# Two transformer layers with product-key experts: the down products with blocks of the v tile standing and 384 activations moving, and the gathered rows summed in SBUF

## The chip, the core and the metric

The kernel runs on one core of one Trainium2 chip. The metric is device time in microseconds (us) of that core, from launch to end; lower is better. The engines are TensorE (PE), VectorE (DVE), ScalarE (ACT), GpSimd (POOL) and SyncE (SP), the last of which only issues transfers here. A column is one element of the free dimension.

## What is computed

The reference is a trunk of two layers. In each layer a mixer sub-layer of three attention branches is followed by PEER, a retrieval of single-neuron experts. The change lies wholly in the last part of PEER. Cut to that:

```python
def peer_ffn(h, w_q, sub_keys, u_tab, v_tab):      # h: 512 tokens x 1024
    ...                       # per token: 8 heads x 16 experts of 16384, with weights g
    u = u_tab[experts]
    vv = v_tab[experts]
    a = gelu(einsum('td,ted->te', xb, u)) * g
    return einsum('te,ted->td', a, vv)
...
x = x + g2 * peer_ffn(...)                          # g2: one factor per model column
```

## The kernel before

The kernel treats the 512 tokens in two ways. For the first 128 tokens (`SPARSE`) it gathers the rows of the chosen experts, 128 a token, with indirect DMAs that POOL issues, and DVE does the arithmetic on them. For the other 384 (`DENSE`) it computes with all 16384 experts: the table comes in 128 tiles of 128 experts x 1024, and the activations, which are zero for experts that weren't chosen once the routing weights are multiplied in, go through PE.

The residual stream `xT` lies with the model dimension on partitions: 8 slices (`KT`) of 128, each with 512 token columns. PSUM has 8 banks of 512 float columns; `PS[4]` and `PS[5]` together are `pair`, which the profile calls `banks4and5`.

To keep precision, each operand of a product is split into a high part in fp32r and the remainder (`_hi`, `_lo`), and `product3` (lines 709 to 714) issues three products: high by high, and the two mixed ones. The helper's lines 712 to 714 are therefore the lines of all products in the profile, of the up stages (names `h_hi`, `u_hi`) and of the down stage (`a_hi`, `u_hi`; the v tiles use the same buffers as the u tiles, so `u_parts` holds v there). The first operand of `product3` is the one that stands in the array (128 partitions x 128 columns), the second the one that moves. In names of the profile and of the listings below, `bank<-moving,standing`.

In the up stages (`query`, `select`, `route`, `rest`) a column is one u tile: 8 slices x 3 products, with a 128x128 block of u standing and the 384 dense activations moving. The results go through Gelu on ACT and out to HBM. The stage `down` then has 16 steps of 8 tiles (`DOWN`), 128 tiles in all. For each tile:

- SP loads the v tile into a slot of `W`, and once per four tiles the activations (`act_in`) and routing weights (`g_cur`).
- ACT rounds the tile (`lead_down`, L1405) and the weighted activations (`round_weighted`, L1411).
- DVE multiplies the next activations by their weights (`weigh`, L2082), takes the remainder of the tile (`u_lo`, L2093), adds one gathered row per sparse token times its weight to a running sum (`sparse_down`, L2072; after it POOL may gather the next row into that place, L1551), and takes the remainder of the activations (`a_lo`, L2097).
- PE (`outputs`, from L1100) waits for both remainders, and issues for each of 3 token blocks x 2 halves of the model dimension one `product3`: 128 tokens stand and 512 columns of v move. The six results accumulate in banks 0 to 3, 6 and 7 (`DENSE_BANKS`) over all 128 tiles, with tokens on partitions.

Four tile buffers let DVE and ACT run ahead of PE by some blocks. The sparse sum lies in `pair`, banks 4 and 5, also with tokens on partitions; DVE clears it (L2060) before the stage.

After the last tile both results have to be turned, since `xT` has the model dimension on partitions. DVE copies the sparse sum to SBUF (L2106), ACT copies the six dense banks (L1446), PE turns 8 + 24 blocks of 128x128 (L1127 and L1135), and DVE adds each, times `g2`, to `xT` (`add_output`, L2110), in 32 instructions of 128 columns. Then all engines meet at a boundary and the next layer begins. The order on every engine is written out by hand; semaphores hold the engines together.

Of the kernel before, what the change touches and what calls it, by code (L numbers as in the profile page):

```python
# [40 lines left out]
ALU = mybir.AluOpType  # L41
ACT = mybir.ActivationFunctionType
# [4 lines left out]
D = 1024  # L47
# [166 lines left out]
def build_trunk(nc, x_t, stream, vecs, consts, c_t, gate_tiles, z_dram, tab_u, tab_v, u_rows, v_rows, out_t, route_dram, act_dram, layers=LAYERS):  # L214
# [3 lines left out]
    with ctx:  # L218
        def sb(name, shape, dt=F32):
            return ctx.enter_context(nc.sbuf_tensor(name, shape, dt))  # L220
# [144 lines left out]
        gathered_rows = sb("gathered_rows", [128, 6, D])  # L365

# [137 lines left out]
        sparse_copied = sem("sparse_copied")  # L504
        sparse_turned = sem("sparse_turned")
        y_ready = sem("y_ready")
        y_copied = sem("y_copied")
        y_turned = sem("y_turned")
# [91 lines left out]

        DENSE_BANKS = [0, 1, 2, 3, 6, 7]
# [104 lines left out]
        def _(pe):  # L706
# [244 lines left out]
            with pe.Fori(0, layers) as layer:  # L951
# [55 lines left out]
                if "experts" in stages:  # L1007
# [92 lines left out]
                    def outputs(step, first=False, last_step=False):  # L1100
                        for j in range(DOWN):
# [3 lines left out]
                            for i, bank in enumerate(DENSE_BANKS):  # L1105
                                t0, d0 = i // 2 * 128, i % 2 * 512
                                if opens and i == 0:
                                    pe.wait_ge(route_copied.sem, route_copied.at("route", layer, STEPS["route"] - 1, Q))
                                    pe.sem_inc(held, 1)
                                if opens and i == 4:  # L1110
                                    pe.wait_ge(col_read.sem, col_read.at("rest", layer, 0, 8))
                                    pe.sem_inc(held, 1)
                                last = product3(PS[bank][:], [a[:, j % 4, t0:t0 + 128] for a in a_parts],
                                                [v[:, j % 4, d0:d0 + 512] for v in u_parts], opens, ends)
                                if ends and i < 5:
                                    last.then_inc(y_ready, 1)
# [7 lines left out]
                    pe.wait_ge(sparse_copied, layer + 1)  # L1124
                    pe.sem_inc(held, 1)
                    for k in range(KT):
                        last = nc.tensor.transpose(pair[:, k * 128:(k + 1) * 128],  # L1127
                                                   gathered_rows[:, 0, k * 128:(k + 1) * 128], cst("ident"))
                    last.then_inc(sparse_turned, 1)
                    for i, bank in enumerate(DENSE_BANKS):  # L1130
                        pe.wait_ge(y_copied, layer * 6 + (i + 1))
                        pe.sem_inc(held, 1)
                        for c in range(4):
                            d0 = i % 2 * 512 + c * 128
                            last = nc.tensor.transpose(PS[bank][:, c * 128:(c + 1) * 128],  # L1135
                                                       gathered_rows[:, 1 + i // 2, d0:d0 + 128], cst("ident"))
                        last.then_inc(y_turned, 1)
# [3 lines left out]
        def _(act):  # L1141
# [127 lines left out]
            with act.Fori(0, layers) as layer:  # L1269
# [44 lines left out]
                if "experts" in stages:  # L1314
# [123 lines left out]
                    act.wait_ge(row_used.sem, row_used.at("summed", layer, STEPS["summed"] - 1, 8))  # L1438
                    act.sem_inc(held, 1)
                    for i, bank in enumerate(DENSE_BANKS):  # L1440
                        if i < 5:
                            act.wait_ge(y_ready, layer * 5 + (i + 1))
                        else:
                            act.wait_ge(col_done.sem, col_done.at("down", layer, STEPS["down"] - 1, DOWN))
                        act.sem_inc(held, 1)
                        fn(gathered_rows[:, 1 + i // 2, i % 2 * 512:i % 2 * 512 + 512], PS[bank][:], ACT.Copy  # L1446
                           ).then_inc(y_copied, 1)
# [139 lines left out]
        def _(dve):  # L1587
# [228 lines left out]
            with dve.Fori(0, layers) as layer:  # L1816
# [85 lines left out]
                if "experts" in stages:  # L1902
# [157 lines left out]
                    nc.vector.memset(pair[:], 0.0).then_inc(sparse_weights, 1)  # L2060
# [6 lines left out]
                    def sparse_down(step, j):  # L2067
# [4 lines left out]
                        stt(pair[:], gather_slot(j), weight[:, ds(step * 8 + j, 1)], pair[:], ALU.mult, ALU.add  # L2072
# [31 lines left out]
                    dve.wait_ge(row_used.sem, row_used.at("summed", layer, STEPS["summed"] - 1, 8))  # L2104
                    dve.sem_inc(held, 1)
                    nc.vector.tensor_copy(gathered_rows[:, 0, :], pair[:]).then_inc(sparse_copied, 1)  # L2106

                    def add_output(k, t0, y):
                        x = xT[:, k, t0:t0 + 128]
                        stt(x, y, modT[:, 5 * KT + k:5 * KT + k + 1], x, ALU.mult, ALU.add)  # L2110

                    dve.wait_ge(sparse_turned, layer + 1)
                    dve.sem_inc(held, 1)
                    for k in range(KT):
                        add_output(k, 0, pair[:, k * 128:(k + 1) * 128])
                    for i, bank in enumerate(DENSE_BANKS):
                        dve.wait_ge(y_turned, layer * 6 + (i + 1))
                        dve.sem_inc(held, 1)
                        for c in range(4):
                            add_output(i % 2 * 4 + c, SPARSE + i // 2 * 128, PS[bank][:, c * 128:(c + 1) * 128])  # L2120
# [191 lines left out]
```

## Time and profile before

| | us |
|---|---|
| median of 3 runs | 4165.5 |
| lowest and highest | 4164.78, 4168.49 |
| span of the profiled execution | 4160.5 |
| PE busy in it | 3785.2 (91%) |
| DVE busy | 2706.0 (65%) |
| ACT busy | 1504.7 (36%) |
| POOL busy | 1562.3 (38%) |

The profiled execution is known by its span, from its first to its last instruction; no other time of it was taken, and what lies around the span is the difference to the runs' median. Products are pipelined: the duration that a row gives to one is longer than the distance from its start to the next one's start, so a busy share near 100% says that PE had no gap, and not how fast it went. The granted clock (PEclk) is 1.00 at 2.4 GHz. The down stage of layer 1 is about from 1553 to 2077 us, that of layer 2 ends at 4144 us.

### The profile page before, as it was taken

The numbers are of one execution on the slowest core, as the hardware profiler recorded it, in microseconds if no ns is written. First come the engines' busy times: TensorE is split into PE (matmuls) and PEld (weight loads), VectorE is DVE, ScalarE is ACT, GpSimd is POOL, SyncE is SP. The second block draws the span as 40 slices with busy tenths as digits, with TensorE's granted clock in tenths as the row PEclk, the third lists the DMA queues.
The fourth block names the chain that finished last, engine by engine and source line by source line (L and its number), as shares of the span: only waits on it lengthen the run. The fifth ranks groups of instructions, "written<-read, shape, count | busy, mean of one in ns | idle before, by whom it ended". The sixth has DMA issues, their size and how long they took to land.

```text
span 4160.5 us, 61961 instructions
## 1 busy us (share of the span) xinstructions
PE 3785.2 (91%) x18366; PEld 3081.0 (74%) x18366; DVE 2706.0 (65%) x5116; ACT 1504.7 (36%) x2412; POOL 1562.3 (38%) x1068
## 2 busy tenths in 40 slices
PE   4788889889999999999948788897999999999998
PEld 3555665389999998888835456653999999988887
DVE  4553333157899868888755543432479998688886
ACT  3224343133444443333333343431334444433332
POOL 2342220045876662222123323200458767522220
PEclk8898999999999999999979999998999999999999
DMA  4341112234779899999634311121447899999995
GB/s 179 127 151 48 58 53 96 78 119 145 252 270 390 344 388 370 356 351 351 242 138 152 127 53 63 60 97 61 138 149 255 298 371 368 383 360 355 355 354 213
DMA packets 340965, 906.71 MB, mean 218 GB/s; under 512 B 28704, under 2 KB 160032, under 8 KB 337312
## 3 DMA queue, kind: packets, MB, share of 16 engines
q1 hardware_dynamic: 215824, 495.33, 33.8%
q0 software_dynamic: 84480, 306.22, 19.9%
q10 hardware_dynamic: 40464, 102.78, 6.3%
q8 instruction: 94, 1.54, 0.1%
q14 instruction: 103, 0.84, 0.1%
HBM read 788.87 MB, written 115.34 MB: 217 GB/s over the span
## 4 chain that ended last, share of the span: by engine, by line
PE 64%; DVE 17%; issue 10%; POOL 3%; ACT 2%; DMA 2%; POOLq 1%; DVEq 1%; ACTq 0%; SPq 0%; PEldq 0%
PE bank L712 16%; PE bank L714 16%; PE bank L713 16%; PE bank L723 8%; DVE arena L2047 3%; PE bank L872 2%; PE bank L843 2%; DVE gathered_rows L1956 2%; DVE arena L2053 2%; DVE arena L1996 1%; POOL u_lo L1543 1%; PE bank L786 1%; DMA W<-stream 1%; PE banks4and L858 1%; DVE arena L1993 1%
## 5 line engine op out<-in xcount | busy, mean ns | idle before, releaser
L1543 POOL TENSOR_TENSOR u_lo<-W,u_hi 128x1024 fp32r<-128x1024 f32 x272 | 688.8, 2534 | 828.4 <-ACT u_hi L1322 825.9
L712 PE MATMUL bank<-h_hi,u_hi 128*128 128x384 f32 (+1 forms) x2176 | 758.8, 349 | 47.3 <-POOL u_lo L1543 47.3
L713 PE MATMUL bank<-h_lo,u_hi 128*128 128x384 f32 (+1 forms) x2176 | 739.6, 340 | 0.0
L714 PE MATMUL bank<-h_hi,u_lo 128*128 128x384 f32 (+1 forms) x2176 | 739.5, 340 | 0.0
L712 PE MATMUL bank<-u_hi,a_hi 128*128 128x512 f32 x1536 | 600.1, 391 | 5.6 <-issue 5.6
L713 PE MATMUL bank<-u_lo,a_hi 128*128 128x512 f32 x1536 | 599.6, 390 | 0.0
L714 PE MATMUL bank<-u_hi,a_lo 128*128 128x512 f32 x1536 | 599.4, 390 | 0.0
L1405 ACT ACTIVATE u_hi<-W 128x1024 fp32r<-128x1024 f32 x256 | 271.7, 1061 | 653.6 <-PE bank L714 635.2
L712 PEld LDWEIGHTS bank<-h_hi,u_hi 128*128 128x128 f32 x2176 | 412.6, 190 | 58.5 <-issue 36.8
L2093 DVE TENSOR_TENSOR u_lo<-W,u_hi 128x1024 fp32r<-128x1024 f32 x256 | 313.7, 1225 | 167.5 <-ACT u_hi L1405 167.4
L713 PEld LDWEIGHTS bank<-h_lo,u_hi 128*128 128x128 f32 x2176 | 412.6, 190 | 5.4
L714 PEld LDWEIGHTS bank<-h_hi,u_lo 128*128 128x128 f32 x2176 | 411.6, 189 | 5.3
L1551 POOL DMA_INDIRECT gathered_rows<-v_rows,arena x192 | 182.9, 952 | 559.2 <-DVE banks4and L2072 537.0
L712 PE MATMUL bank<-hH,mix_high 128*128 128x512 f32 x672 | 297.5, 443 | 82.3 <-POOLq L521 42.1
L1322 ACT ACTIVATE u_hi<-W 128x1024 fp32r<-128x1024 f32 x272 | 287.8, 1060 | 171.3 <-ACT act_out L1336 151.3
L712 PEld LDWEIGHTS bank<-u_hi,a_hi 128*128 128x128 f32 x1536 | 289.4, 188 | 66.4 <-issue 6.2
L713 PEld LDWEIGHTS bank<-u_lo,a_hi 128*128 128x128 f32 x1536 | 289.5, 188 | 60.2
L714 PEld LDWEIGHTS bank<-u_hi,a_lo 128*128 128x128 f32 x1536 | 289.4, 188 | 60.2
L713 PE MATMUL bank<-hL,mix_high 128*128 128x512 f32 x672 | 274.7, 409 | 0.0
L1956 DVE SCALAR_TENSOR_TENSOR gathered_rows<-gathered_rows,banks4and 128x1024 f32<-128x1024 f32 x192 | 231.0, 1216 | 32.2 <-DMA gathered_rows<-u_rows,arena 32.1
L1336 ACT ACTIVATE act_out<-bank 128x384 f32<-128x384 f32 x256 | 125.5, 490 | 343.9 <-PE bank L714 293.4
L2072 DVE SCALAR_TENSOR_TENSOR banks4and<-gathered_rows,arena,banks4and 128x1024 f32<-128x1024 f32 x192 | 246.2, 1282 | 0.0
(209 smaller groups left out, 6346.7 us busy)
## 6 DMA issues: line engine op xcount, KB each, us to landing
W<-tab_u SPq DMA_DIRECT2D x256, 512.0 KB, 4.1
W<-tab_v SPq DMA_DIRECT2D x256, 512.0 KB, 8.5
W<-stream SPq DMA_DIRECT2D x206, 512.0 KB, 4.9
act_scratch<-act_out ACTq DMA_DIRECT2D x256, 192.0 KB, 4.3
route_scratch<-arena ACTq DMA_DIRECT2D x24, 2048.0 KB, 11.8
act_in<-act_scratch SPq DMA_DIRECT2D x64, 768.0 KB, 6.8
g_cur<-route_scratch SPq DMA_DIRECT2D x64, 768.0 KB, 10.8
gate_raw<-gate_tiles POOLq DMA_DIRECT2D x48, 512.0 KB, 3.8
```

The source lines that it names most:

```text
L712: mm(out, w[0], a[0], start=first, stop=False)
L713: mm(out, w[0], a[1], start=False, stop=False)
L714: return mm(out, w[1], a[0], start=False, stop=last)
L723: last = mm(out, w[:, k * pitch + off:k * pitch + off + width], act[:, k, :], start=(k == 0), stop=(k == kts - 1))
L1322: fn(u_parts[0][:, u_buffer(stage, n), :], raw, ACT.Copy).then_inc(col_hi.sem, 1)
L1336: fn(act_out[:, n % 2, :], PS[6 + n % 2][:, 0:DENSE], ACT.Gelu).then_inc(col_read.sem, 1)
L1405: fn(u_parts[0][:, j % 4, :], raw, ACT.Copy).then_inc(col_hi.sem, 1)
L1543: nc.gpsimd.tensor_tensor(u_parts[1][:, b, :], raw, u_parts[0][:, b, :].bitcast(F32), ALU.subtract).then_inc(col_lo.sem, 1)
L1551: nc.gpsimd.indirect_dma_start(gather_slot(k), None, u_rows if k < SPARSE else v_rows, bass.IndirectOffsetOnAxis(ap=row[:, k % SPARSE:k % ...
L1956: stt(gather_slot(k), gather_slot(k), 1.0, pair[:], ALU.mult, ALU.mult, accum_out=dots[:, k:k + 1]).then_inc(row_used.sem, 1)
L2072: stt(pair[:], gather_slot(j), weight[:, ds(step * 8 + j, 1)], pair[:], ALU.mult, ALU.add).then_inc(row_used.sem, 1)
L2093: tt(u_parts[1][:, j % 4, :], raw, u_parts[0][:, j % 4, :].bitcast(F32), ALU.subtract).then_inc(v_lo_done.sem, 1)
```

## The change

`outputs` swaps the roles of the two operands. For each of the 8 slices of the model dimension, a 128x128 block of the v tile stands, and the 384 dense activations move. There are 24 products of 384 columns for each tile, where there were 18 of 512. The results lie in columns 128 to 511 of all 8 banks, with the model dimension on partitions, as in `xT`. So `pair` is no longer free for the sparse sum, which moves to a new SBUF tensor, `sparse_sum`. At the end PE turns its 8 blocks into columns 0 to 127 of the same banks, and DVE adds each bank, 512 columns, to a slice of `xT`. The copies by DVE and ACT and the 24 dense transposes are gone, with their semaphores.

```diff
+        sparse_sum = sb("sparse_sum", [128, D])
...
                             opens, ends = first and j == 0, last_step and j == DOWN - 1
-                            for i, bank in enumerate(DENSE_BANKS):
-                                t0, d0 = i // 2 * 128, i % 2 * 512
-                                if opens and i == 0:
+                            for k in range(KT):
+                                if opens and k == 0:
                                     pe.wait_ge(route_copied.sem, route_copied.at("route", layer, STEPS["route"] - 1, Q))
                                     pe.sem_inc(held, 1)
-                                if opens and i == 4:
+                                if opens and k == 4:
+                                    pe.wait_ge(row_used.sem, row_used.at("late", layer, 0, 8))
+                                    pe.sem_inc(held, 1)
+                                if opens and k == 6:
                                     pe.wait_ge(col_read.sem, col_read.at("rest", layer, 0, 8))
                                     pe.sem_inc(held, 1)
-                                last = product3(PS[bank][:], [a[:, j % 4, t0:t0 + 128] for a in a_parts],
-                                                [v[:, j % 4, d0:d0 + 512] for v in u_parts], opens, ends)
-                                if ends and i < 5:
-                                    last.then_inc(y_ready, 1)
+                                last = product3(PS[k][:, SPARSE:T], [v[:, j % 4, k * 128:(k + 1) * 128] for v in u_parts],
+                                                [a[:, j % 4, :] for a in a_parts], opens, ends)
                             last.then_inc(col_done.sem, 1)
...
-                    pe.wait_ge(sparse_copied, layer + 1)
+                    pe.wait_ge(row_used.sem, row_used.at("summed", layer, STEPS["summed"] - 1, 8))
                     pe.sem_inc(held, 1)
                     for k in range(KT):
-                        last = nc.tensor.transpose(pair[:, k * 128:(k + 1) * 128],
-                                                   gathered_rows[:, 0, k * 128:(k + 1) * 128], cst("ident"))
-                    last.then_inc(sparse_turned, 1)
-                    for i, bank in enumerate(DENSE_BANKS):
-                        pe.wait_ge(y_copied, layer * 6 + (i + 1))
-                        pe.sem_inc(held, 1)
-                        for c in range(4):
-                            d0 = i % 2 * 512 + c * 128
-                            last = nc.tensor.transpose(PS[bank][:, c * 128:(c + 1) * 128],
-                                                       gathered_rows[:, 1 + i // 2, d0:d0 + 128], cst("ident"))
-                        last.then_inc(y_turned, 1)
+                        nc.tensor.transpose(PS[k][:, 0:SPARSE], sparse_sum[:, k * 128:(k + 1) * 128], cst("ident")
+                                            ).then_inc(y_ready, 1)
...
-                    for i, bank in enumerate(DENSE_BANKS):
...
-                        fn(gathered_rows[:, 1 + i // 2, i % 2 * 512:i % 2 * 512 + 512], PS[bank][:], ACT.Copy
-                           ).then_inc(y_copied, 1)
...
-                    nc.vector.memset(pair[:], 0.0).then_inc(sparse_weights, 1)
+                    nc.vector.memset(sparse_sum[:], 0.0).then_inc(sparse_weights, 1)
...
-                        stt(pair[:], gather_slot(j), weight[:, ds(step * 8 + j, 1)], pair[:], ALU.mult, ALU.add
+                        stt(sparse_sum[:], gather_slot(j), weight[:, ds(step * 8 + j, 1)], sparse_sum[:], ALU.mult, ALU.add
                             ).then_inc(row_used.sem, 1)
...
-                    nc.vector.tensor_copy(gathered_rows[:, 0, :], pair[:]).then_inc(sparse_copied, 1)
-
-                    def add_output(k, t0, y):
-                        x = xT[:, k, t0:t0 + 128]
-                        stt(x, y, modT[:, 5 * KT + k:5 * KT + k + 1], x, ALU.mult, ALU.add)
...
+                        dve.wait_ge(y_ready, layer * KT + (k + 1))
                         dve.sem_inc(held, 1)
-                        for c in range(4):
-                            add_output(i % 2 * 4 + c, SPARSE + i // 2 * 128, PS[bank][:, c * 128:(c + 1) * 128])
+                        stt(xT[:, k, :], PS[k][:], modT[:, 5 * KT + k:5 * KT + k + 1], xT[:, k, :], ALU.mult, ALU.add)
```

The instructions of PE at the beginning of one block (one v tile) of the down stage, before:

```order
L1102 REGISTER_ALU
L712 MATMUL bank0<-u_hi,a_hi 128x512
L713 MATMUL bank0<-u_lo,a_hi 128x512
L714 MATMUL bank0<-u_hi,a_lo 128x512
L712 MATMUL bank1<-u_hi,a_hi 128x512
L713 MATMUL bank1<-u_lo,a_hi 128x512
L714 MATMUL bank1<-u_hi,a_lo 128x512
L712 MATMUL bank2<-u_hi,a_hi 128x512
L713 MATMUL bank2<-u_lo,a_hi 128x512
L714 MATMUL bank2<-u_hi,a_lo 128x512
```

And the same place of the changed kernel, whose line numbers are five lower:

```order
L1097 REGISTER_ALU
L707 MATMUL bank0<-a_hi,u_hi 128x384
L708 MATMUL bank0<-a_lo,u_hi 128x384
L709 MATMUL bank0<-a_hi,u_lo 128x384
L707 MATMUL bank1<-a_hi,u_hi 128x384
L708 MATMUL bank1<-a_lo,u_hi 128x384
L709 MATMUL bank1<-a_hi,u_lo 128x384
L707 MATMUL bank2<-a_hi,u_hi 128x384
L708 MATMUL bank2<-a_lo,u_hi 128x384
L709 MATMUL bank2<-a_hi,u_lo 128x384
```

Each product keeps its bank for three in a row; before, six banks follow one another in a block, now eight.

The end of the down stage on PE, from the last product on, before (`C` is the identity, which moves; the block to be turned stands):

```order
L714 MATMUL bank7<-u_hi,a_lo 128x512
L1124 REGISTER_ALU
L1127 MATMUL banks4and5<-C,gathered_rows 128x128 x8
L1131 ISA
L1135 MATMUL bank0<-C,gathered_rows 128x128 x4
L1131 REGISTER_ALU
L1135 MATMUL bank1<-C,gathered_rows 128x128 x4
L1131 REGISTER_ALU
L1135 MATMUL bank2<-C,gathered_rows 128x128 x4
L1131 REGISTER_ALU
L1135 MATMUL bank3<-C,gathered_rows 128x128 x4
L1131 REGISTER_ALU
```

And in the changed kernel:

```order
L709 MATMUL bank7<-a_hi,u_lo 128x384
L1119 REGISTER_ALU
L1122 MATMUL bank0<-C,sparse_sum 128x128
L1122 MATMUL bank1<-C,sparse_sum 128x128
L1122 MATMUL bank2<-C,sparse_sum 128x128
L1122 MATMUL bank3<-C,sparse_sum 128x128
L1122 MATMUL banks4and5<-C,sparse_sum 128x128 x2
L1122 MATMUL bank6<-C,sparse_sum 128x128
L1122 MATMUL bank7<-C,sparse_sum 128x128
```

Of 32 transposes 8 are left, each of which now goes to a bank of its own, and the semaphore instructions between groups of four are gone.

The end of the down stage on DVE, from its last remainder on, before:

```order
L2097 TENSOR_TENSOR a_lo<-act_in,a_hi 128x384
L2104 REGISTER_ALU
L2106 COPY gathered_rows<-banks4and5 128x1024
L2110 SCALAR_TENSOR_TENSOR xT<-banks4and5,modT,xT 128x128 x8
L2117 ISA
L2110 SCALAR_TENSOR_TENSOR xT<-bank0,modT,xT 128x128 x4
L2117 REGISTER_ALU
L2110 SCALAR_TENSOR_TENSOR xT<-bank1,modT,xT 128x128 x4
L2117 REGISTER_ALU
L2110 SCALAR_TENSOR_TENSOR xT<-bank2,modT,xT 128x128 x4
L2117 REGISTER_ALU
L2110 SCALAR_TENSOR_TENSOR xT<-bank3,modT,xT 128x128 x4
```

And in the changed kernel, where lines 2081 and 2083 are the wait and the addition:

```order
L2073 TENSOR_TENSOR a_lo<-act_in,a_hi 128x384
L2081 ISA
L2083 SCALAR_TENSOR_TENSOR xT<-bank0,modT,xT 128x512
L2081 REGISTER_ALU
L2083 SCALAR_TENSOR_TENSOR xT<-bank1,modT,xT 128x512
L2081 REGISTER_ALU
L2083 SCALAR_TENSOR_TENSOR xT<-bank2,modT,xT 128x512
L2081 REGISTER_ALU
L2083 SCALAR_TENSOR_TENSOR xT<-bank3,modT,xT 128x512
L2081 REGISTER_ALU
```

The copy of the sparse sum is gone, and 32 additions of 128 columns have become 8 of 512, each with a wait of its own.

## Rows read from the trace of the kernel before

**Rows 1.** Chain that ended last: shares by engine and by line.

```profile
PE 64%; DVE 17%; issue 10%; POOL 3%; ACT 2%; DMA 2%; POOLq 1%; DVEq 1%; ACTq 0%; SPq 0%; PEldq 0%
PE bank L712 16%; PE bank L714 16%; PE bank L713 16%; PE bank L723 8%; DVE arena L2047 3%; PE bank L872 2%; PE bank L843 2%; DVE gathered_rows L1956 2%; DVE arena L2053 2%; DVE arena L1996 1%; POOL u_lo L1543 1%; PE bank L786 1%; DMA W<-str
```

**Rows 2.** Busy time by stretch: down stage, last up columns, part of down.

```profile
core 0: us, PE busy (x) PEld busy (x) DVE busy (x) ACT busy (x) POOL busy (x), PEclk, DMA share, GB/s
1553.00:2077.00 524.00, 523.93 (x2305) 433.75 (x2306) 426.48 (x508) 188.23 (x257) 113.14 (x119) 1.00 0.94 337
1541.50:1549.50 8.00, 8.00 (x48) 8.00 (x47) 3.45 (x4) 2.99 (x4) 2.53 (x3) 1.00 1.06 403
1600.00:1700.00 100.00, 100.00 (x443) 82.83 (x442) 82.14 (x99) 36.63 (x50) 23.86 (x25) 1.00 1.01 357
```

**Rows 3.** Timeline, last block of layer 2: start us, us, engine, line.

```profile
4139.67 0.39 PE L714 MATMUL bank<-u_hi,a_lo 128*128 128x512 f32 x1
...
4143.75 0.39 PE L714 MATMUL bank<-u_hi,a_lo 128*128 128x512 f32 x1
```

**Rows 4.** Timeline of PE, last up columns of layer 1.

```profile
1541.08 0.34 PE L714 MATMUL bank<-h_hi,u_lo 128*128 128x384 f32 x1
...
1549.92 0.34 PE L714 MATMUL bank<-h_hi,u_lo 128*128 128x384 f32 x1
```

**Rows 5.** Timeline of PE, beginning of the down stage, both layers.

```profile
1553.07 0.76 PE L712 MATMUL bank<-u_hi,a_hi 128*128 128x512 f32 x1 [2.81 <-issue]
...
1555.76 0.63 PE L712 MATMUL bank<-u_hi,a_hi 128*128 128x512 f32 x1
...
3619.36 0.63 PE L713 MATMUL bank<-u_lo,a_hi 128*128 128x512 f32 x1
...
3624.05 0.63 PE L712 MATMUL bank<-u_hi,a_hi 128*128 128x512 f32 x1
```

**Rows 6.** Timeline, end of the down stage in layer 1.

```profile
2076.75 0.39 PE L714 MATMUL bank<-u_hi,a_lo 128*128 128x512 f32 x1
2076.98 1.03 PE L1127 MATMUL banks4and<-C,gathered_rows 128*128 128x128 f32 x8
...
2078.18 2.16 DVE L2110 SCALAR_TENSOR_TENSOR xT<-banks4and,modT,xT 128x128 f32<-128x128 f32 x8 [12.20 <-PE banks4and L1127]
...
2080.25 6.28 DVE L2110 SCALAR_TENSOR_TENSOR xT<-bank,modT,xT 128x128 f32<-128x128 f32 x24
```

**Rows 7.** Groups, 1580 to 2080 us: busy us, mean ns.

```profile
L2093 DVE TENSOR_TENSOR u_lo<-W,u_hi 128x1024 fp32r<-128x1024 f32 x119 | 145.9, 1226 | 81.2 <-ACT u_hi L1405 81.2
...
L712 PEld LDWEIGHTS bank<-u_hi,a_hi 128*128 128x128 f32 x730 | 137.0, 188 | 28.4
...
L2072 DVE SCALAR_TENSOR_TENSOR banks4and<-gathered_rows,arena,banks4and 128x1024 f32<-128x1024 f32 x90 | 115.4, 1283 | 0.0
...
L2097 DVE TENSOR_TENSOR a_lo<-act_in,a_hi 128x384 fp32r<-128x384 f32 x120 | 66.1, 551 | 0.0
```

**Rows 8.** Lines of DVE: least, median, greatest ns, first, last start.

```profile
L2060 DVE MEMSET banks4and<- x2: 912/912/912, 1529.7 to 3594.0; 128x1024 f32 x2
...
L2063 DVE TENSOR_TENSOR arena<-arena x2: 274/1261/2248, 1530.6 to 3594.8; 128x128 f32<-128x128 f32 x2
...
L2082 DVE TENSOR_TENSOR act_in<-act_in,g_cur x256: 544/552/562, 1544.8 to 4123.6; 128x384 f32<-128x384 f32 x128
```

**Rows 9.** Lines, same columns: a transpose, two widths on DVE.

```profile
L1127 PE MATMUL banks4and<-C,gathered_rows x16: 271/272/273, 2077.0 to 4144.7; 128*128 128x128 f32 x16
...
L2053 DVE TENSOR_TENSOR arena<-arena,bank x192: 681/683/687, 1217.9 to 3569.8; 128x512 f32<-128x512 f32 x192
...
L2047 DVE TENSOR_TENSOR arena<-arena,bank x192: 1212/1216/1223, 1215.7 to 3567.6; 128x1024 f32<-128x1024 f32 x192
```

**Rows 10.** Timeline of POOL and DVE, down stage of layer 1.

```profile
1702.07 0.95 POOL L1551 DMA_INDIRECT gathered_rows<-v_rows,arena  x1 [3.13 <-DVE banks4and L2072]
...
1702.92 1.23 DVE L2093 TENSOR_TENSOR u_lo<-W,u_hi 128x1024 fp32r<-128x1024 f32 x1 [0.73 <-ACT u_hi L1405]
```

More of the change, by code:

```diff
@@ L503, in build_trunk @@
         sparse_weights = sem("sparse_weights")
-        sparse_copied = sem("sparse_copied")
-        sparse_turned = sem("sparse_turned")
         y_ready = sem("y_ready")
-        y_copied = sem("y_copied")
-        y_turned = sem("y_turned")
         vector_chain = signal("vector_chain", VECTOR_LINKS)
@@ L599, in gather_place @@
                     return stage, (k - first) // width, (k - first) % width
-        DENSE_BANKS = [0, 1, 2, 3, 6, 7]
         def key_tiles(stage, i):
@@ L1436, in _ @@
                     splits(STEPS["down"] - 1, last=True)
-                    act.wait_ge(row_used.sem, row_used.at("summed", layer, STEPS["summed"] - 1, 8))
-                    act.sem_inc(held, 1)
-                    for i, bank in enumerate(DENSE_BANKS):
[L1441 to L1445, printed above, removed]
-                        fn(gathered_rows[:, 1 + i // 2, i % 2 * 512:i % 2 * 512 + 512], PS[bank][:], ACT.Copy
-                           ).then_inc(y_copied, 1)
                     for b in range(2):
@@ L2103, in _ @@
                     split(STEPS["down"] - 1, last_step=True)
-                    dve.wait_ge(row_used.sem, row_used.at("summed", layer, STEPS["summed"] - 1, 8))
-                    dve.sem_inc(held, 1)
-                    nc.vector.tensor_copy(gathered_rows[:, 0, :], pair[:]).then_inc(sparse_copied, 1)
-                    def add_output(k, t0, y):
-                        x = xT[:, k, t0:t0 + 128]
-                        stt(x, y, modT[:, 5 * KT + k:5 * KT + k + 1], x, ALU.mult, ALU.add)
-                    dve.wait_ge(sparse_turned, layer + 1)
-                    dve.sem_inc(held, 1)
                     for k in range(KT):
-                        add_output(k, 0, pair[:, k * 128:(k + 1) * 128])
-                    for i, bank in enumerate(DENSE_BANKS):
-                        dve.wait_ge(y_turned, layer * 6 + (i + 1))
+                        dve.wait_ge(y_ready, layer * KT + (k + 1))
                         dve.sem_inc(held, 1)
-                        for c in range(4):
-                            add_output(i % 2 * 4 + c, SPARSE + i // 2 * 128, PS[bank][:, c * 128:(c + 1) * 128])
+                        stt(xT[:, k, :], PS[k][:], modT[:, 5 * KT + k:5 * KT + k + 1], xT[:, k, :], ALU.mult, ALU.add)
                     leave(dve)
```

## The prediction

> **What bounds the kernel now.** I read the chain of work that ended last first, because a change of products only matters where TensorE (PE) sets the pace. PE holds 64% of that chain, and its three largest entries are the three lines of the helper that issues products [rows 1]. These lines serve the up stages and the down stage alike, so the next view is busy time by stretch. Over the whole down stage of layer 1, 524 us long, PE is busy 523.93 us with 2305 products, at a granted clock of 1.00; in a stretch inside it PE has no gap at all [rows 2]. The DMA share is as high as 1.01 there, so the queues deserve a rival below, but nobody on PE waits for them.
>
> The unit in which to price the change is the pitch from one product's start to the next, not the modelled duration (0.39 us against a pitch of some 0.227). From 4139.67 to 4143.75 us PE starts 18 products, exactly one block of the v tile: 4.08 us, 226.7 ns each [rows 3]. At 2.4 GHz 512 columns take 213.3 ns, so each product carries 13.3 ns that doesn't depend on its columns, if that is how the time splits. A second row decides it: in the last up columns ("rest"), whose shape is 128x128 standing and 384 moving, the very shape of the changed products, 51 starts lie between 1541.08 and 1549.92 us, so 173.3 ns each, which is 160 + 13.3 [rows 4]. This stretch has full clock and no gap [rows 2]. Both shapes pay the same fixed 13.3 ns.
>
> At the beginning of the stage PE waits 2.8 us, starts at half clock, and a 512 product then has a pitch of 426.4 ns (3619.36 to 3624.05 us is eleven products), 512 columns at 1.2 GHz with nothing on top [rows 5]. This slow stretch is a matter of some 3 to 6 us in each layer.
>
> Behind the last product of the stage stands a tail in which PE no longer sets the pace. In layer 1 the last product starts at 2076.75; the transposes of the sparse sum follow at 2076.98, VectorE (DVE) adds from 2078.18, and works without a gap through 8 and then 24 small pieces until 2080.25 + 6.28 = 2086.53 [rows 6]. From the last product's start to the last addition: 9.78 us. The ACT copies and the second set of transposes lie beside DVE's additions and are not on the path.
>
> **The change, part by part.**
>
> Products. A block goes from 6 banks x 3 = 18 products of 512 columns to 8 x 3 = 24 of 384. Both move 9216 columns, so only the fixed part counts: 24 x 173.3 = 4.160 us against 18 x 226.7 = 4.080, that is 6 x 13.3 ns = 0.080 us more. There are 128 blocks in a layer: 10.24 us a layer, 20.5 us in both. In the slow stretch, where the 512 row shows nothing on top of the columns, a block of either form costs the same (24 x 320 = 18 x 426.7 = 7.68 us). Some 9 us of both layers run so, a little over one block, which takes off 0.1 us. Sum +20.4.
>
> The size of the fixed part is what the whole forecast hangs on, so I bound it by rows. Row reading: 0.01 us in 8.84 over 51 pitches is 0.2 ns, times 6144 products is 1.2 us. The low end is 160 ns, the half of what 384 columns take at the half clock. The high end is the weight load's own duration, 188 ns [rows 7]. I take 173.3, since the row is of the same shape, type and clock.
>
> Waits at the start. The new first block waits for the sparse up rows to be used (banks 4 and 5) ahead of its fifth bank, and for the last column to be read ahead of its seventh. DVE used the last sparse up row before its memset, at 1529.7 in layer 1 [rows 8], 23 us before the first down product: nothing. The last column's bank was awaited before the fifth bank already, and is now awaited after 18 products and not 12: nothing, or a gain hidden under PE's own start. The first product waits for the same two signals as before. Moving the memset to SBUF costs nothing: it takes 0.91 us, and DVE's next work for the down stage comes at 1544.8 (L2082) [rows 8].
>
> The sparse sum in SBUF. Per block DVE does 1.226 (u_lo), 1.283 (the sum), 0.551 (a_lo) and 0.552 (weighting) = 3.61 us [rows 7, 8], against 4.08 us of PE now and 4.16 then. The sum reads and writes PSUM today. A DVE instruction of 1024 columns with one input in each memory takes 1.216 (L2047), with both inputs in SBUF 1.226 (L2093) [rows 7, 9], so I price the new one at 1.23, range 1.21 to 1.28. Either way it is behind PE's cover of 0.5 us a block, and is worth nothing.
>
> Tail. The PSUM copy by DVE, the six ACT copies and the 24 transposes go; the copy was ahead of the last product anyway. Now: last product, 0.173 us to the first transpose, 0.272 for one transpose [rows 9], and 0.17 us from the end of a transpose to DVE's start (2078.01 to 2078.18, [rows 6]); DVE begins 0.62 us after the last product's start, against 1.43 now. The seven other transposes arrive every 0.109 us (1.03 less 0.272, over 7), far quicker than DVE needs them. DVE then has 8 pieces of 512 columns. The pitch of the small ones is (6.28 - 0.34) / 23 = 0.258 us at 128 columns. From 512 to 1024 columns a DVE instruction grows by 1.216 - 0.683 = 0.533 us [rows 9], so 384 more columns are 0.400: pitch 0.658, last piece 0.74, together 7 x 0.658 + 0.74 = 5.35 us. Tail 5.97, against 9.78: 3.8 us less a layer, 7.6 in both. Bounds: 8 halves of 1.216 give 4.86, and no overlap at all 8 x 0.744 = 5.95, so 3.2 to 4.3 a layer. The next layer's start then moves as one piece, since every engine waits for the same boundary.
>
> Sum: +20.4 - 7.6 = +12.8 us. The profiled span is 4160.5 us, 5.0 less than the median of the runs shown (4165.5), and I carry that difference over: 4173.3 in the trace, **4178.3 us** in the timed runs, 0.31% slower.
>
> **The rivals.**
>
> Less fixed cost in the new form: the other side. The 13.3 ns might belong to something that the down stage sheds, such as DVE's writes to PSUM beside it, or might shrink over eight banks. For it: at half clock it is absent [rows 5], so it isn't a constant of the product. Against it: the rest columns pay it though DVE makes only four instructions in the 8 us [rows 2]. The turning point is near: 12.8 us over 6144 products is 2.1 ns, so below 11.2 ns the change is a gain; below 12.6 ns it is within 0.2%. At the low end, 160 ns, it would be 24 x 0.0133 x 256 = 82 us less than forecast, 4096. I give 6 in 100, a third of it beyond the turning point.
>
> The Trainium skill, "TensorE: Matmul & The Clock Gate", Back-to-back issue gap, gives a warm product by itself its columns at 2.4 GHz plus about 2.5 ns. By that figure for the new form alone the change would end at 4112, and for both forms at 4162. The trace shows 13.3 ns at both widths and does not agree with it, so the measurement decides.
>
> The stage is held by its transfers. The DMA share of 0.94 over the stage and 1.01 inside it speaks for it. Then the extra PE time would hide in waits, and only the tail is left: 4165.5 - 7.6 = 4158. Against it: PE has no gap between 1600 and 1700, and in the up stage the same engines moved 403 GB/s against 357 here [rows 2]. 3 in 100.
>
> PE falls back to the weight loads, or to DVE. If each product waited for its load of 188 ns: 14.7 ns x 6144 = +90 us, 4268. In the rest columns the loads fill PE's load side wholly (8.00 of 8.00 us) and the pitch still is 173.3. DVE is the likelier culprit: the new sum has two inputs in SBUF, and an instruction of that kind, only 128x128, once took 2.25 us while POOL's subtraction ran (L2063, against 0.27 in layer 2) [rows 8]. In the down stage POOL has only its gathers, 0.95 us each. Each waits for the end of a sum (the releaser in its row), so it can't overlap that one, and the u_lo subtraction that overlaps them by 0.1 us keeps its 1.23 [rows 10]. If each sum were stretched by a whole gather, DVE would need 3.61 + 0.95 = 4.56 us: +0.40 x 256 = +102, 4281. It decides from 0.55 us of stretch on. The Trainium skill, "SBUF — State Buffer", Who interferes with whom, states that a DVE instruction with two SBUF inputs contends with a GpSimd instruction that reads SBUF, and not with one that only writes; the L2063 row agrees. Both together 5 in 100.
>
> The tail gives nothing: the eight wide additions or their waits take as long as the 32 small ones. 4165.5 + 20.4 = 4186. 4 in 100.
>
> **How the numbers follow.** The forecast has 82 in 100. Its own range: 1.2 us for reading the pitch, 1.1 a layer for the tail, some 2 us for where the slow stretch ends (it was 3 us long in one layer and 6 in the other, and half of it is lost), and about 2 us between medians. That gives 4173 to 4184; with a part of the nearest cases 4172 to 4185. A measurement of this kernel tells 0.2%, 8.3 us, from no change. Faster than that: 0.03 (the first rival's far part and a little). Within: 0.09 (the rest of that rival, the transfers, and the forecast's lowest edge). Slower: 0.88.
>
> **What the changed profile would show.** In the down stage 24 products of 384 to a block and a block every 4.16 us, no gap on PE, the ACT wait on PE longer; DVE's sum at about 1.23 us. The stage of a layer from 523.7 to 533.9 us. In the tail DVE starting 0.6 us after the last product and 8 pieces in 5.3 us. Wrong would be: a pitch other than 173.3, gaps on PE released by DVE or DMA, or a DVE sum beyond 1.8 us.

## The result and the profile after

The changed kernel takes 4177.6 us (median of 10 runs, 4174.8 to 4184.9) against 4165.7 (10 runs, 4159.7 to 4178.1): ratio 1.0031, 95% interval 1.0021 to 1.0040, so between 9 and 17 us slower, 11.9 by the medians. The forecast was 4178.3, slower, with 4172 to 4185, and +12.8 us as the sum of its parts.

The first view is again busy time by stretch, for the down stage of layer 1 and 100 us inside it (PE busy, PEld the weight loads, DVE, ACT, POOL, then clock, DMA share, GB/s):

```profile
core 0: us, PE busy (x) PEld busy (x) DVE busy (x) ACT busy (x) POOL busy (x), PEclk, DMA share, GB/s
1547.00:2081.00 534.00, 533.63 (x3070) 533.66 (x3071) 426.25 (x508) 185.73 (x253) 115.62 (x119) 1.00 0.93 330
1600.00:1700.00 100.00, 100.00 (x578) 100.00 (x578) 80.71 (x96) 35.52 (x50) 23.16 (x25) 1.00 0.98 347
```

It answers to [rows 2]: PE still has no gap once it has started at 1547.37, the stage is 10 us longer, and the traffic has fallen from 337 to 330 GB/s because the same bytes take more time. The load side is busy all the time now, where it was 83%, which might look like a new bound; the pitch below says that it isn't.

PE's timeline, at the beginning of the stage in both layers and then from the last product of the last tile but one to the last product, start us first; the last two rows frame the half-clock stretch of layer 2:

```profile
1547.37 0.66 PE L707 MATMUL bank<-a_hi,u_hi 128*128 128x384 f32 x1 [2.97 <-issue]
1547.83 0.52 PE L708 MATMUL bank<-a_lo,u_hi 128*128 128x384 f32 x1
...
1550.39 0.50 PE L707 MATMUL bank<-a_hi,u_hi 128*128 128x384 f32 x1
...
2077.17 0.33 PE L709 MATMUL bank<-a_hi,u_lo 128*128 128x384 f32 x1
...
2081.33 0.34 PE L709 MATMUL bank<-a_hi,u_lo 128*128 128x384 f32 x1
...
3625.98 0.61 PE L707 MATMUL bank<-a_hi,u_hi 128*128 128x384 f32 x1 [2.65 <-issue]
...
3629.53 0.34 PE L709 MATMUL bank<-a_hi,u_lo 128*128 128x384 f32 x1
```

A tile is 2081.33 - 2077.17 = 4.16 us for 24 products, 173.3 ns each, against 4.08 in [rows 3]. At half clock eight products lie between 1547.83 and 1550.39: 320.0 ns, 384 columns at 1.2 GHz with nothing on top, as the 512 row in [rows 5]. From the first to the last product it is 533.96 us in layer 1; before, from 1553.07 to 2076.75, 523.68. That is +10.28, where the prediction had 10.24 less some 0.05 for the half-clock stretch.

The tail of layer 1, which answers to [rows 6], and below it the groups of DVE and ACT between 1580 and 2080 us, which answer to [rows 7]:

```profile
2081.51 0.60 PE L1122 MATMUL bank<-C,sparse_sum 128*128 128x128 f32 x4
2081.93 2.73 DVE L2083 SCALAR_TENSOR_TENSOR xT<-bank,modT,xT 128x512 f32<-128x512 f32 x4 [12.88 <-PE bank L1122]
...
2084.57 1.40 DVE L2083 SCALAR_TENSOR_TENSOR xT<-banks4and,modT,xT 128x512 f32<-128x512 f32 x2
2085.89 1.40 DVE L2083 SCALAR_TENSOR_TENSOR xT<-bank,modT,xT 128x512 f32<-128x512 f32 x2
```

```profile
L2069 DVE TENSOR_TENSOR u_lo<-W,u_hi 128x1024 fp32r<-128x1024 f32 x118 | 144.7, 1226 | 91.0 <-ACT u_hi L1391 90.9
...
L1391 ACT ACTIVATE u_hi<-W 128x1024 fp32r<-128x1024 f32 x117 | 124.2, 1062 | 314.4 <-PE bank L709 314.4
L2048 DVE SCALAR_TENSOR_TENSOR sparse_sum<-gathered_rows,arena,sparse_sum 128x1024 f32<-128x1024 f32 x90 | 115.1, 1279 | 0.0
```

DVE starts 0.60 us after the last product's start and ends at 2085.89 + 1.40 = 2087.29: the tail is 5.96 us, against 9.78. The sum in SBUF takes 1.279 us against 1.283 in PSUM. The chain of waits is the old one: ACT waits for PE (309.0 us in this window before, 314.4 now), DVE for ACT, and PE for nobody.

Where the 12.4 us between the two spans (4160.5 and 4172.9) lie: down stage +10.28 and +9.01, tails -3.82 and -3.81, sum +11.7. In layer 2 the stage grew by less because its half-clock stretch had been longer in the kernel before. There it ended at about this row:

```profile
3624.89 0.40 PE L714 MATMUL bank<-u_hi,a_lo 128*128 128x512 f32 x1
```

From 3618.80 to this start lie 14 products in 6.09 us, 2.92 more than at 226.7 ns; in the changed kernel 11 lie between 3625.98 and 3629.53, 3.55 us, 1.64 more than at 173.3. The difference of 1.28 us is that between +10.28 and +9.01. The remaining +0.7 is the sum of two larger differences in stages that the change does not touch: 5.7 us less ahead of layer 1's down stage, and 6.4 us more between the two. Such differences come without a change of code: over all traces of this case the down stage of layer 1 starts between 1544.27 and 1553.07 us, and from the end of its tail to the down stage of layer 2 it takes 1532.3 to 1543.8. The spread of one kernel's runs, 10 to 18 us, agrees with that.

### The profile page after: what moved, and what is told of

Read it like the earlier page. It is cut to its first block, busy times and chain, and to the rows that moved or that the text cites. A ratio compares the mean times of both kernels' runs of the same rounds, so it can differ in the third digit from the quotient of the medians.

```text
span 4172.9 us, 64829 instructions
## 1 busy us (share of the span) xinstructions
PE 3798.6 (91%) x19854; PEld 3274.0 (78%) x19854; DVE 2696.2 (65%) x5066; ACT 1497.6 (36%) x2400; POOL 1567.7 (38%) x1068
## 4 chain that ended last, share of the span: by engine, by line
PE 64%; DVE 17%; issue 10%; POOL 2%; ACT 2%; DMA 2%; POOLq 1%; DVEq 1%; ACTq 0%; SPq 0%; PEldq 0%
PE bank L707 14%; PE bank L709 14%; PE bank L708 14%; PE bank L718 8%; DVE arena L2023 3%; PE bank L867 2%; PE banks4and L707 2%; PE banks4and L709 2%; PE banks4and L708 2%; DVE gathered_rows L1932 2%; PE bank L838 2%; DVE arena L2029 2%; DVE arena L1972 1%; PE bank L781 1%; DMA W<-stream 1%
## 5 line engine op out<-in xcount | busy, mean ns | idle before, releaser
L707 PE MATMUL bank<-a_hi,u_hi 128*128 128x384 f32 x1536 | 515.3, 335 | 5.6 <-issue 5.6
L708 PE MATMUL bank<-a_lo,u_hi 128*128 128x384 f32 x1536 | 514.8, 335 | 0.0
L709 PE MATMUL bank<-a_hi,u_lo 128*128 128x384 f32 x1536 | 514.7, 335 | 0.0
L707 PEld LDWEIGHTS bank<-a_hi,u_hi 128*128 128x128 f32 x1536 | 289.5, 189 | 6.2 <-issue 6.2
L708 PEld LDWEIGHTS bank<-a_lo,u_hi 128*128 128x128 f32 x1536 | 289.7, 189 | 0.0
L709 PEld LDWEIGHTS bank<-a_hi,u_lo 128*128 128x128 f32 x1536 | 289.5, 188 | 0.0
L2023 DVE TENSOR_TENSOR arena<-arena,bank 128x1024 f32<-128x1024 f32 x192 | 232.7, 1212 | 20.1 <-PE bank L1084 19.0
```

What stands on the lines that cost most here:

```text
L707: mm(out, w[0], a[0], start=first, stop=False)
L708: mm(out, w[0], a[1], start=False, stop=False)
L709: return mm(out, w[1], a[0], start=False, stop=last)
L2023: tt(onehots[:, :, q % 4], pickT[:, 0:2, four:four + 4].unsqueeze(3).broadcast_to([128, 2, 4, 128]), iota.unsqueeze(1).unsqueeze(1).broadc ...
```

## The experiments

The theory: at full clock every product of these 4-byte operands costs 13.3 ns beyond its columns, so 6 more products a tile cost 20.5 us, while the 8 wide additions give 7.6 back. The rivals: the loss comes from the new roles or the eight banks; from the weight loads; from the sum in SBUF. The listings show the lines of an edit that matter; `...` stands for what is left out.

**The count alone, e1.** Old roles and old tail, two of the six banks in halves, so 24 products a tile.

```diff
-    last = product3(PS[bank][:], [a[:, j % 4, t0:t0 + 128] for a in a_parts],
-                    [v[:, j % 4, d0:d0 + 512] for v in u_parts], opens, ends)
+    pieces = ((0, 256), (256, 256)) if i < 2 and not (opens or ends) else ((0, 512),)
+    for c0, wide in pieces:
+        last = product3(PS[bank][:, c0:c0 + wide], [a[:, j % 4, t0:t0 + 128] for a in a_parts],
+                        [v[:, j % 4, d0 + c0:d0 + c0 + wide] for v in u_parts], opens, ends)
```

> The kernel before, with the activations still standing, but two of the six banks computed in halves of 256 columns in 126 of the 128 tiles: 24 products per tile as in the changed kernel, with the old roles, banks and tail. Fixed part per product: 6 x 13.3 ns x 252 tiles = +20.2 us, 4185.9 where before is 4165.7. If the loss of the change came from what stands and what moves, or from eight banks: no change, 4165.7. If a product can't follow faster than its weight load's 188 ns: twelve products of 256 columns wait for it, +0.9 us a tile, 4391.

Measured: 4189.2 us, ratio 1.0064 (1.0051 to 1.0078), +22.6 us by the medians of the same chip (4166.6). PE's timeline over one tile:

```profile
1700.01 0.28 PE L712 MATMUL bank<-u_hi,a_hi 128*128 128x256 f32 x1
...
1701.45 0.40 PE L712 MATMUL bank<-u_hi,a_hi 128*128 128x512 f32 x1
...
1702.83 0.39 PE L712 MATMUL bank<-u_hi,a_hi 128*128 128x512 f32 x1
...
1704.19 0.28 PE L712 MATMUL bank<-u_hi,a_hi 128*128 128x256 f32 x1
```

Twelve halves take 1.44 us, 120.0 ns each, which is 106.7 + 13.3. The six wide ones behind them take 1.38 us, 230 ns each, and the last six 1.36, the usual 226.7. So a tile is 4.18 and not 4.16: the count explains the loss, with 0.02 us a tile more for the change of width.

**The same count and width in the old roles, e9.**

```diff
-    last = product3(PS[bank][:], [a[:, j % 4, t0:t0 + 128] for a in a_parts],
-                    [v[:, j % 4, d0:d0 + 512] for v in u_parts], opens, ends)
+    for _ in range(2 if i < 2 and not (opens or ends) else 1):
+        wide = 512 if opens or ends else 384
+        last = product3(PS[bank][:, 0:wide], [a[:, j % 4, t0:t0 + 128] for a in a_parts],
+                        [v[:, j % 4, d0:d0 + wide] for v in u_parts], opens, ends)
```

> The kernel before with the activations standing, its six banks and its old tail, but 24 products of 384 columns in 126 of the 128 tiles: each bank gets only the first 384 columns of its 512, and the first two banks get them twice, so the model columns beyond are left out and the sums of two banks are doubled. Exactly the count and width of the changed kernel in the old roles. If only count and width matter: a tile 4.160 us, +20.2 us, 4186. If the roles or the eight banks of the changed kernel cost or save something: a tile other than 4.16 us, by as much.

```profile
1699.93 0.33 PE L712 MATMUL bank<-u_hi,a_hi 128*128 128x384 f32 x1
...
1704.09 0.33 PE L712 MATMUL bank<-u_hi,a_hi 128*128 128x384 f32 x1
```

The second start is the same product one tile later: 24 products in 4.16 us, to the hundredth that of the changed kernel. The time is 4187.4 us, ratio 1.0048 (1.0031 to 1.0065). What stands, what moves, and whether six or eight banks take turns makes no difference to the pitch that the trace can show.

**The sum alone in SBUF, e3.**

```diff
+        sparse_sum = sb("sparse_sum", [128, D])
...
-    stt(pair[:], gather_slot(j), weight[:, ds(step * 8 + j, 1)], pair[:], ALU.mult, ALU.add
+    stt(sparse_sum[:], gather_slot(j), weight[:, ds(step * 8 + j, 1)], sparse_sum[:], ALU.mult, ALU.add
```

> The kernel before with only the sparse sum moved to SBUF; products and tail as before. Prediction's step: hidden, 4165.7 within 2 us, DVE's sum about 1.28 us (as in the changed kernel) and a block still 4.08 us. Rival: gathers and the sum with two SBUF inputs disturb each other, a DVE sum well over 1.28 us and gaps on PE.

Measured: 4165.4 us, ratio 1.0000 (0.9991 to 1.0010). DVE's sum, least, median and greatest ns:

```profile
L2073 DVE SCALAR_TENSOR_TENSOR sparse_sum<-gathered_rows,arena,sparse_sum x192: 1276/1279/1283, 1553.3 to 4132.9; 128x1024 f32<-128x1024 f32 x192
```

The step is free. It says little on two inputs in SBUF beside a gather, because a gather waits for a sum and seldom runs beside one: of the 128 sums of layer 1 only 4 overlap one by more than 0.05 us, and they take 1.278 us too. The remainder of the tile (`u_lo`), which also has both inputs in SBUF, overlaps one 114 times, by 0.18 us in the mean, and keeps its 1.225 us. By the contention rule of the Trainium skill ("SBUF — State Buffer", Who interferes with whom) a gather would have to read SBUF through the shared port to disturb it, and no run here shows that it does.

**How narrow, e2 and e2b.** All six banks in two pieces, of 256 and 256, or of 384 and 128 columns: the edit of e1 without `i < 2`, and with `((0, 384), (384, 128))`.

> The kernel before with all six banks in halves of 256 columns in 126 of 128 tiles: 36 products a tile. Fixed part per product: pitch 106.7 + 13.3 = 120 ns, a tile 4.32 us, +60 us, 4226. If the weight load of 188 ns sets the pitch: a tile 6.77 us, +677 us, 4843. A floor of some 109 ns, as between the transposes, would not show here.

> The kernel before with all six banks in pieces of 384 and 128 columns in 126 of 128 tiles: also 36 products a tile. Fixed part alone: pitches 173.3 and 66.7 ns, 4.32 us a tile, 4226, the same as with halves. A floor of some 109 ns for the narrow products (the pitch of the transposes): a tile 18 x 0.282 = 5.08 us, +252 us, 4418. A pitch of 188 for both: 4843.

Measured (one run each): 4229.0 and 4441.7 us beside 4164.6, where 4226 and 4418 were expected. PE in e2:

```profile
1700.21 0.28 PE L712 MATMUL bank<-u_hi,a_hi 128*128 128x256 f32 x1
...
1704.41 0.28 PE L714 MATMUL bank<-u_hi,a_lo 128*128 128x256 f32 x1
```

These are 35 products in 4.20 us, 120.0 ns each: the fixed part again, though a load of 192 ns belongs to each and the load side is busy throughout. So the load's duration is not what a product waits for. In e2b one tile's 36 products take 5.18 us:

```profile
1699.97 0.39 PE L712 MATMUL bank<-u_hi,a_hi 128*128 128x384 f32 x1
...
1705.15 0.39 PE L712 MATMUL bank<-u_hi,a_hi 128*128 128x384 f32 x1
```

With 173.3 ns for the wide ones, the narrow ones cost (5.18 - 18 x 0.1733) / 18 = 114 ns each, where the fixed part alone would give 66.7. That is a mean. Behind the six products of one bank the trace has pitches of 233, 174 and 174 ns (384 columns) and 60, 112 and 111 ns (128 columns), so part of what the narrow ones cost shows behind the first wide one. The floor of some 109 ns that the transposes had shown holds roughly.

**Which operands pay, e8 and e10, timed again as e11 and e12.** The products read the upper half of each element as bf16. The listing is the edit of the changed kernel (e8, e11); e10 and e12 do the same to the kernel before, with its roles.

```diff
-    [v[:, j % 4, k * 128:(k + 1) * 128] for v in u_parts], [a[:, j % 4, :] for a in a_parts]
+    [v[:, j % 4, k * 128:(k + 1) * 128].bitcast(BF16)[:, 1::2] for v in u_parts],
+    [a[:, j % 4, :].bitcast(BF16)[:, 1::2] for a in a_parts]
```

> The changed kernel, but the down products read both operands as bf16: the upper two bytes of each fp32r element, so the lower bits are left out; columns, counts and order are the same. If the 13.3 ns belong to 4-byte operands (in the standing or the moving one), the pitch falls towards 160 to 163 ns, a tile to 3.9 us, and the time by about 66 us to 4111. If they belong to every product, 173.3 ns and 4177.6 stay.

> The kernel before with its down products reading the upper two bytes of each fp32r element as bf16 (the lower bits are left out), 18 products of 512 columns as before. The same edit on the changed kernel took the pitch from 173.3 to 168.9 ns. If the 4.4 ns are a saving per product: a pitch of 222.2 ns, a tile 4.00 us, -20 us, 4145. If it is a saving per column (4.4 ns on 384): 5.9 ns on 512, a pitch of 220.8, -27 us, 4139.

Measured (one run each): 4148.6 for the changed kernel so edited, 4158.0 for the kernel before, so both expectations missed: the first saved 29 us and not 66, the second 6 (beside 4163.5) and not 20 to 27. The timelines of PE in layer 1, first e8, then e10:

```profile
1699.92 0.33 PE L707 MATMUL bank<-a_hi,u_hi 128*128 128x384 bf16 x1
...
1706.00 0.33 PE L707 MATMUL bank<-a_hi,u_hi 128*128 128x384 bf16 x1
```

```profile
1700.30 0.39 PE L712 MATMUL bank<-u_hi,a_hi 128*128 128x512 bf16 x1
...
1712.45 0.39 PE L712 MATMUL bank<-u_hi,a_hi 128*128 128x512 bf16 x1
```

36 pitches of 168.9 ns, and 54 of 225.0. Here, in layer 1, the 128 columns between the two widths take 56 ns, where 53.3 would be the clock's, and hardly 1 ns is left that doesn't grow with them. A tile is 4.05 us in both forms. If this held for the whole run, the count would cost nothing, and the sign of the change would turn:

> The changed kernel with bf16 views (e8) again, now timed beside the old products with bf16 views (e12). In their single looks the pitches were 168.9 ns for 384 columns and 224.9 for 512, so a tile would be 24 x 168.9 = 4.05 us here and 18 x 224.9 = 4.05 there: with these operands the count of products costs nothing, and only the tail's 7.6 us is left. Expected 6 to 8 us below e12, the other sign than with 4-byte operands. If the count costs 13.3 ns a product here too: 12.8 us above e12.

> The kernel before with bf16 views (e10) again, timed: a tile 18 x 224.9 = 4.05 us, so 256 x 0.03 = 8 us below the kernel before, some 4157; e11 6 to 8 us below this one.

Measured: e11 4147.2 us, ratio to the kernel before 0.9962 (0.9949 to 0.9976); e12 4158.5, ratio 0.9981 (0.9971 to 0.9991). The changed form is some 8 us faster by the ratios and 11 by the medians; the two intervals overlap a little, so the traces are wanted as well. They show that the expectation was right in layer 1 alone. In layer 2 e12 looks like this (start of the stage and one tile; below it a group of its weight loads between 1580 and 2060 us, in layer 1, with a mean of 96 ns):

```profile
3619.49 0.39 PE L712 MATMUL bank<-u_hi,a_hi 128*128 128x512 bf16 x1 [3.48 <-issue]
...
3699.73 0.39 PE L712 MATMUL bank<-u_hi,a_hi 128*128 128x512 bf16 x1
...
3703.81 0.39 PE L712 MATMUL bank<-u_hi,a_hi 128*128 128x512 bf16 x1
```

```profile
L712 PEld LDWEIGHTS bank<-u_hi,a_hi 128*128 128x128 bf16 x712 | 68.4, 96 | 91.8
```

A tile of 18 products takes 4.08 us there, 226.7 ns each, as with 4-byte operands, and so it does through the whole stage, in e10 too; e8 and e11 keep 168.9 ns in both layers. Why the layers of e10 and e12 differ is open; in both traces the stage of layer 1 begins at half clock, and that of layer 2 at full clock. From the first to the last product e11 takes 519.99 and 520.12 us, e12 519.57 and 522.01; the tails are 5.95 against 9.78 us. Together that is 9.1 us for the changed form. The sign turned, mostly by the tails, and in layer 2 because the wide products gained nothing from the views.

A load takes 96 ns with the views, half of the 188 before, while the pitch of 384 columns fell by 4.4 ns only. That again says that the loads don't set it.

**The tail.** e7 cuts the eight additions of the changed kernel into 32. e4 keeps the 18 products of 512 and gives them wide additions. e5 starts the changed kernel's additions inside the last tile.

```diff
 # e4, PE: four transposes fill a bank for each slice k; dense banks finish in the order 0, 2, 6, 1, 3, 7
...
+    for k in range(KT):
+        if k % 4 == 0:
+            pe.wait_ge(y_copied, layer * 6 + (3 if k < 4 else 6))
+            pe.sem_inc(held, 1)
+        target, c = PS[TURNED_BANKS[k]], slice(k * 128, (k + 1) * 128)   # [4, 5, 0, 2, 6, 1, 3, 7]
+        for n in range(4):
+            last = nc.tensor.transpose(target[:, n * 128:(n + 1) * 128], gathered_rows[:, n, c], cst("ident"))
+        last.then_inc(y_turned, 1)
...
 # e5, PE: in the last tile, behind each bank's three products
+    nc.tensor.transpose(PS[k][:, 0:SPARSE], sparse_sum[:, k * 128:(k + 1) * 128], cst("ident")).then_inc(y_ready, 1)
...
 # e7, DVE
+    for t0 in range(0, T, 128):
+        stt(xT[:, k, t0:t0 + 128], PS[k][:, t0:t0 + 128], modT[:, 5 * KT + k:5 * KT + k + 1],
+            xT[:, k, t0:t0 + 128], ALU.mult, ALU.add)
```

> The changed kernel with its eight additions of 512 columns in the tail cut into 32 of 128. The prediction's tail: 0.62 + 31 x 0.258 + 0.34 = 8.96 us against 5.96, +3.0 a layer, +6.0 in all, 4183.6. Rival: the additions are hidden, the tail stays at 5.96 us.

> The kernel before with its 18 products of 512 and a new tail: banks of the first model half computed first in each tile, the 32 transposes gathered four to a bank for each slice of the model dimension, and 8 additions of 512 columns on DVE. Tail from the last product's start: 0.23 to the first transpose, 0.44 for the four, some 0.35 to DVE's start, 5.35 of additions = 6.4 us against 9.78, so -3.4 a layer, -6.8 in all: 4158.9. Rival: the last bank's copy on ACT and its transposes come too late and DVE waits for them between its fourth and fifth piece, so that half or all of the gain is lost: 4162 to 4166.

> The changed kernel, with the transpose of each sparse block issued right behind the last three products of its bank, so that DVE adds bank after bank while PE still computes the others. The first addition starts some 0.96 us into the last tile, and eight take 5.35: the end is 6.3 us after the last tile's start against 3.99 + 5.96 = 9.95 now. -3.6 a layer, -7.3 in all: 4170.3 where the changed kernel has 4177.6 and before 4165.7. Rival: the tail is not on the path, no change, 4177.6.

| | us | ratio to before | tail or last tile in layer 1 |
|---|---|---|---|
| e7 | 4183.1, one run (expected 4183.6) | | 8.95 us from the last product (expected 8.96) |
| e4 | 4159.5 (expected 4158.9) | 0.9984 (0.9975 to 0.9994) | 6.34 us from the last product (expected 6.4) |
| e5 | 4170.9 (expected 4170.3) | 1.0014 (1.0005 to 1.0023) | 6.29 us from the last tile's start (expected 6.3) |

DVE in e7, whose last product starts at 2081.64 us:

```profile
2082.23 4.23 DVE L2084 SCALAR_TENSOR_TENSOR xT<-bank,modT,xT 128x128 f32<-128x128 f32 x16 [12.88 <-PE bank L1122]
2086.38 2.15 DVE L2084 SCALAR_TENSOR_TENSOR xT<-banks4and,modT,xT 128x128 f32<-128x128 f32 x8
2088.44 2.15 DVE L2084 SCALAR_TENSOR_TENSOR xT<-bank,modT,xT 128x128 f32<-128x128 f32 x8
```

DVE in e5, whose last tile starts at 2077.92 us and whose last product starts at 2082.74:

```profile
2078.85 2.73 DVE L2087 SCALAR_TENSOR_TENSOR xT<-bank,modT,xT 128x512 f32<-128x512 f32 x4 [9.23 <-PE bank L1118]
...
2082.81 1.40 DVE L2087 SCALAR_TENSOR_TENSOR xT<-bank,modT,xT 128x512 f32<-128x512 f32 x2
```

The timeline of e4 from the last product on:

```profile
2072.90 0.39 PE L715 MATMUL bank<-u_hi,a_lo 128*128 128x512 f32 x1
2073.13 1.03 PE L1134 MATMUL banks4and<-C,gathered_rows 128*128 128x128 f32 x8
2073.88 1.41 DVE L2110 SCALAR_TENSOR_TENSOR xT<-banks4and,modT,xT 128x512 f32<-128x512 f32 x2 [11.76 <-PE banks4and L1134]
2074.00 2.78 PE L1134 MATMUL bank<-C,gathered_rows 128*128 128x128 f32 x24
2075.21 4.03 DVE L2110 SCALAR_TENSOR_TENSOR xT<-bank,modT,xT 128x512 f32<-128x512 f32 x6
```

DVE goes from its first to its eighth addition without a gap, and ends at 2079.24. The last ACT copy and the transposes of the second half hide beside it. e4 beats both kernels: it has the cheap products of the one and nearly the tail of the other. e5 moves the changed kernel by -6.7 us against its own 4177.6, close to the expected -7.3, and still leaves it above the kernel before: no tail can pay back 20 us.

## Why the prediction was right

- **What bounds the stage.** PE without a gap, in both kernels and in every experiment's stage that was looked at. Shown.
- **Products, +20.4.** A tile of 4.16 us as forecast; +10.28 and +9.01 measured, 19.3 in both. The piece that missed is the half-clock stretch of layer 2, which cost 1.3 us less than before: the prediction had named its end as uncertain by 2 us. That the columns' count and not the roles decide is shown by e9, and the fixed part at a third width by e2.
- **Waits at the start.** PE's gap was 2.97 and 2.65 us, before 2.81 in layer 1: nothing, as said. No gap shows at the new wait ahead of bank 4 either: its first product starts at 1551.08 us, 0.17 behind its predecessor.
- **The sum in SBUF.** Free, shown by e3. The price taken, 1.23, was the low side of its range; it is 1.279, as the operation in PSUM was.
- **The tail, -7.6.** 5.96 us against a forecast of 5.97, and the mechanism (DVE's additions by their number) is shown by e7 and e4 from both sides.
- **The rivals.** A smaller fixed cost in the new form did not come; the turning point at 11.2 ns was near, and with bf16 views, where 24 products of 384 columns take no longer than 18 of 512, the kernel did turn. The transfers never held PE. The weight loads fill their side wholly and yet set no pitch at 384 or 256 columns.
- **One step was reasoned badly.** The prediction took the 5.0 us between the profiled span and the median for time that lies around the span, and carried it over. In the run with both numbers the time around the span is 1.9 us (4174.84 over 4172.9), so the rest was, as far as can be told, that one execution being 3 us below the median. It did no harm, partly by luck, since the profiled execution of the changed kernel was 2.7 us below its median as well: the forecast of the trace was 4173.3, and 4172.9 came by luck within 0.4, with differences of -5.7 and +6.4 us in untouched stages.

## What to carry to other kernels

Where PE has no gap, price a reshaping of products by pitch, and look for a row of the new shape elsewhere in the same trace: here another stage had run 384 columns with a 128x128 block standing, and its 173.3 ns decided the question to within 1 us. At equal columns, fewer and wider products won here with 4-byte operands; how the result lies then decides only the tail, and a tail of many small additions can be widened without touching the products. A gain outside the loop of 8 us weighs little against 0.08 us in a loop of 256.

## What the runs showed of the hardware

- With fp32r operands the pitch at full clock was 120.0, 173.3 and 226.7 ns for 256, 384 and 512 columns: the columns at 2.4 GHz plus 13.3 ns, the same for all. At half clock it was 320.0 and 426.4 for 384 and 512, with no fixed part. Two products that share the standing block (lines 707 and 708) were no cheaper than others; each has a weight load of its own in the trace (3071 loads to 3070 products).
- With every second bf16 element of the same buffers it was 168.9 ns for 384 in both layers, and for 512 it was 225.0 ns in layer 1 and 226.7 in layer 2. Only the two of layer 1 agree in an excess of 5.5% that grows with the columns. The Trainium skill, "TensorE: Matmul & The Clock Gate", Back-to-back issue gap, gives 2.5 ns beyond the columns for a warm product by itself; neither form here agrees. Whether the step of two elements or the type makes the difference stays open: no contiguous bf16 operand was tried.
- A weight load took 188 to 192 ns with 4-byte operands and 96 ns with the bf16 views; neither set the pitch at 256 columns or more.
- Products of 128 columns cost about 114 ns in the mix with 384, and the first six products of 512 columns after halves took 230 ns each. The cause is not settled.
- After PE's gap ahead of the down stage (2.65 to 3.5 us), the pitch was that of half clock for some 2.5 to 6 us, by execution and layer. In layer 2 of e5 (gap 2.99 us) and e12 (3.48 us) there was no such stretch: the granted clock was 1.00 from the first product.
